# A decoder layer on one core: the first expert group's gather, and the last quarter of the output projection, cut into smaller steps

## The reference

```python
merged = gates[:, :, 0] * br_pool + gates[:, :, 1] * br_rwkv + gates[:, :, 2] * br_nsa
x = x + merged @ w_out[l]                      # the output projection
h = rms_norm(x, norm_ffn[l])
x = x + hier_moe(h, ...)                       # router, 32 experts
return rms_norm(x, norm_final)
# in hier_moe: best of 4 groups, best 2 of its 8 experts per token, then
hid = jax.nn.silu(h @ w_gate[e]) * (h @ w_up[e])
y = y + combine[..., e:e + 1] * (hid @ w_down[e])
```

## Time and profile before

| | us |
|---|---|
| median of three runs | 683.96 |
| profiled execution | 684.78 |
| its span | 683.0 |
| TensorE busy | 613.2 (90%) |
| VectorE busy | 235.7 (35%) |
| ScalarE busy | 139.6 (20%) |
| bytes moved | 158.94 MB, mean 233 GB/s |

### The profile page before, as it was taken

How to read it: one execution, slowest core, us unless ns; L and a number is a source line. 1 busy time by engine, 2 the same in 40 slices (tenths; PEclk the granted TensorE clock), 3 DMA queues, 4 the chain that set the end, 5 groups by cost and what they waited for, 6 DMA issues and landing times.

```text
span 683.0 us, 11651 instructions
## 1 busy us (share of the span) xinstructions
PE 613.2 (90%) x4900; PEld 445.8 (65%) x4900; DVE 235.7 (35%) x597; ACT 139.6 (20%) x345; POOL 22.6 (3%) x25
## 2 busy tenths in 40 slices
PE   5999999999999999999999999995888984948684
PEld 5888887888877767787778888885244441414232
DVE  2151548334254665346300222235223231213123
ACT  2110242131434442345311000001110010010013
POOL 1000000002200021000000000000000000000000
PEclk9999999999999999999999999996999997979796
DMA  9484335712201110111149964884899999999992
GB/s 346 153 323 151 124 126 190 301 62 101 87 2 64 63 63 2 63 65 54 70 164 425 421 230 176 339 342 181 341 420 418 421 419 422 421 422 421 422 390 103
DMA packets 27143, 158.94 MB, mean 233 GB/s; under 512 B 2880, under 2 KB 7120, under 8 KB 9168
## 3 DMA queue, kind: packets, MB, share of 16 engines
q1 hardware_dynamic: 24368, 139.28, 52.0%
q10 hardware_dynamic: 2720, 18.88, 6.6%
HBM read 157.07 MB, written 1.07 MB: 232 GB/s over the span
## 4 chain that ended last, share of the span: by engine, by line
PE 65%; issue 32%; ACT 1%; DVE 1%; DMA 1%; POOL 0%; SPq 0%; POOLq 0%; ACTq 0%; DVEq 0%
PE bank L601 46%; PE bank L799 5%; PE bank L897 3%; PE bank L926 2%; PE bank L946 2%; PE bank L956 1%; PE bank L910 1%; DMA table<-params 1%; PE bank L1016 1%; PE bank L831 1%; PE bank L622 1%; PE bank L861 1%; PE bank L966 1%; PE bank L850 1%; ACT ring L1482 0%
## 5 line engine op out<-in xcount | busy, mean ns | idle before, releaser
L601 PE MATMUL bank<-hT,ring 128*128 128x256 f32 (+2 forms) x960 | 216.4, 378 | 4.3 <-ACTq L1318 4.3
L601 PEld LDWEIGHTS bank<-hT,ring 128*128 128x128 f32 (+2 forms) x960 | 173.6, 190 | 37.7 <-issue 17.6
L601 PE MATMUL bank<-yT,ring 128*128 128x256 f32 x256 | 55.4, 379 | 0.0
L601 PEld LDWEIGHTS bank<-yT,ring 128*128 128x128 f32 x256 | 48.6, 190 | 6.6
L1180 PE MATMUL bank<-ring,work 128*32 128x512 f32 (+1 forms) x148 | 37.5, 680 | 16.1 <-DMA work<-experts 7.2
L1306 ACT ACTIVATE work<-bank 128x512 f32<-128x512 f32 (+1 forms) x43 | 21.8, 508 | 130.5 <-PE bank L1152 58.3
L1632 DVE TENSOR_TENSOR tok<-tok,bank 128x512 f32<-128x512 f32 (+1 forms) x34 | 22.3, 656 | 74.2 <-PE bank L1188 74.2
L1147 PEld LDWEIGHTS bank<-work 128*128 128x128 f32 x256 | 32.1, 205 | 5.5 <-issue 3.3
L1160 PE MATMUL bank<-ring,work 128*32 128x512 f32 x280 | 33.1, 594 | 1.6 <-DMA ring<-experts 1.6
L1147 PE MATMUL bank<-work 128*128 128x128 f32 x256 | 32.3, 288 | 2.0 <-DVEq L2099 2.0
L1188 PE MATMUL bank<-work 128*128 128x512 f32 (+1 forms) x68 | 33.0, 620 | 0.8 <-ACT work L1306 0.8
(11 more groups left out here) (244 smaller groups left out, 719.7 us busy)
## 6 DMA issues: line engine op xcount, KB each, us to landing
ring<-front SPq DMA_DIRECT2D x48, 1024.0 KB, 4.8
ring<-experts SPq DMA_DIRECT2D x44, 1024.0 KB, 26.5
ring<-experts ACTq DMA_DIRECT2D x8, 1024.0 KB, 11.9
table<-experts SPq DMA_DIRECT2D x6, 1024.0 KB, 26.5
yT<-experts SPq DMA_DIRECT2D x6, 1024.0 KB, 26.3
work<-experts SPq DMA_DIRECT2D x6, 1024.0 KB, 26.2
hT<-experts SPq DMA_DIRECT2D x4, 1024.0 KB, 25.5
xcmp<-experts SPq DMA_DIRECT2D x3, 1024.0 KB, 27.6
```

Source lines behind the costliest of these rows:

```text
L601: return first(pe.matmul(o, l, r, start=(k == 0), stop=(k == n - 1)))
```

## The change

Two places are rewritten.

*Last quarter.* Its tile 1 gets a PSUM bank of its own (`outlast`). VectorE adds and squares the two tiles in turn, each by itself. The transposes go into two banks, tile 0 and tile 1 apart; tile 0's are multiplied by the gain on ScalarE, tile 1's on VectorE, and `route(3)` waits for both.

*First group.* Each block's gather is followed by the gate and up products of the block before it, so the two kinds alternate. The blocks go to banks 0 and 1 in turn; ScalarE, not VectorE, multiplies each by the gain, one block at a time. The waits for `xn` and for free banks stand ahead of the one for the seats. The seats' weights are turned after the products, and ScalarE's copy of them comes after its tanh. Groups 1 to 7 keep their order; in all groups `taken` now rises with the last product of a chunk.

```diff
-        hand("out3", 7), hand("hT22", 2), hand("hT23", 3)
+        hand("out3", 7), hand("hT22", 2), hand("outlast", 6), hand("hT23", 3), hand("hTlast", 0)
...
+            def turn_last(i, name):
+                pe.wait_ge(q["sum_ready"], 4 + i)
+                o = begin(name)
+                for b in range(2):
+                    last = first(pe.transpose(o[:, b * P:(b + 1) * P], tok[:, i, (6 + b) * P:(7 + b) * P], ident))
+                end(last, name)
...
             route(2)
-            turn_sum(3)
+            turn_last(0, "hT23")
+            turn_last(1, "hTlast")
             end(route(3), "router")
...
+                def gate_up(gang, k):
+                    w = weights(gang * GCH + k).rearrange("p (e n) -> p e n", e=GANG)
+                    for e in range(GANG):
+                        last = pe.matmul(bank[2][CAP * e:CAP * (e + 1), :], gath[:, k, CAP * e:CAP * (e + 1)],
+                                         w[:, e, :], start=(k == 0), stop=(k == KD - 1))
+                    if k < KD - 1:
+                        last.then_inc(taken, 1)
+                    return last
...
+                pe.wait_ge(q["xn2_ready"], NT)
+                for j in range(8):
+                    pe.wait_ge(bank_free[j], before_loop[j])
+                pe.wait_ge(q["sel_ready"], 1)
+                for k in range(KD + 1):
+                    if k < KD:
+                        gather(bank[k % 2][:, k // 2 * P:(k // 2 + 1) * P], k).then_inc(q["gathered"], 1)
+                    if k:
+                        pe.wait_ge(q["gath_ready"], k)
+                        last = gate_up(0, k - 1)
...
# ScalarE, ahead of its xn copies
+            b0 = full(act, "hT23")
+            for k in (6, 7):
+                ins = copy(hT[:, k, 0:P], b0[:, (k - 6) * P:(k - 5) * P], scale=pr("g_ffn")[:, k:k + 1])
+            give(ins, "hT_odd_ready", "hT23")
# ScalarE, gathered_experts
+                for k in range(KD):
+                    act.wait_ge(q["gathered"], k + 1)
+                    copy(gath[:, k, :], bank[k % 2][:, k // 2 * P:(k // 2 + 1) * P], scale=pr("g_ffn")[:, k:k + 1])\
+                        .then_inc(q["gath_ready"], 1)
...
# VectorE
-            for n in range(4):
+            for n in range(3):
...
+            for i, name in enumerate(("out3", "outlast")):
+                b0 = full(dve, name)
+                o = tok[:, i, 768:D]
+                chain(stt(o, b0[:, i * 256:(i + 1) * 256], 0.5, o, ALU.mult, ALU.add), "sum_ready")
+                dve.sem_inc(bank_free[plan[name][0]], 1)
+                squares(o, stat[:, 27 + 4 * i:28 + 4 * i], at=256 * i)
...
-            sum_turned(3)
+            b0 = full(dve, "hTlast")
+            chain(tt(hT[:, 6:8, P:S], b0[:, 0:2 * P].rearrange("p (k t) -> p k t", k=2),
+                     like(pr("g_ffn")[:, 6:8, None], [P, 2, P]), ALU.mult), "hT_ready")
+            dve.sem_inc(bank_free[plan["hTlast"][0]], 1)
```

More of the change, by code:

```diff
@@ L1061, in output @@
                 w = chunk(C_OUT + n).rearrange("p (k c) -> p k c", k=KD)
-                o = begin(f"out{n}") if 0 in tiles else bank[plan[f"out{n}"][0]]
+                name = "outlast" if tiles == (1,) else f"out{n}"
+                o = begin(name)
                 for i in tiles:
@@ L1067, in output @@
                         last = mm(o[:, i * 256:(i + 1) * 256], merged[:, k, i * P:(i + 1) * P], w[:, k, :], k, KD)
+                end(last, name)
                 if 1 in tiles:
-                    end(last, f"out{n}")
                     pe_take()
@@ L1079, in turn_sum @@
                 end(last, f"hT2{n}")
+            def turn_last(i, name):
+                pe.wait_ge(q["sum_ready"], 4 + i)
+                o = begin(name)
+                for b in range(2):
+                    last = first(pe.transpose(o[:, b * P:(b + 1) * P], tok[:, i, (6 + b) * P:(7 + b) * P], ident))
+                end(last, name)
             def route(n):
+                if n == 3:
+                    pe.wait_ge(q["hT_odd_ready"], 3)
                 pe.wait_ge(q["hT_ready"], 2 + n + 1)
@@ L1134, in gathered_experts, with gather, turn_weights @@
             def gathered_experts():
[L1137 to L1149, removed]
+                def gate_up(gang, k):
[6 more added lines that the diff above has]
+                    return last
+                def gather(o, k):
+                    for i in range(NT):
+                        last = pe.matmul(o, xn[:, i, k * P:(k + 1) * P], sel[:, i, :], start=(i == 0), stop=(i == 1))
+                    return last
+                def turn_weights(gang):
                     pe.wait_ge(q["wsel_ready"], gang + 1)
@@ L1153, in gathered_experts @@
                     last.then_inc(q["wsel_turned"], 1)
[L1155 to L1163, removed]
+                pe.wait_ge(q["xn2_ready"], NT)
[8 more added lines that the diff above has]
+                        last = gate_up(0, k - 1)
+                for gang in range(NGANG):
+                    if gang:
+                        pe.wait_ge(q["sel_ready"], gang + 1)
+                        for b in range(2):
+                            for kk in range(4):
+                                last = gather(bank[b][:, kk * P:(kk + 1) * P], 4 * b + kk)
+                            last.then_inc(q["gathered"], 1)
+                        turn_weights(gang)
+                        for k in range(KD):
+                            if k % 4 == 0:
+                                pe.wait_ge(q["gath_ready"], KD + (gang - 1) * 2 + (k // 4 + 1))
+                            last = gate_up(gang, k)
                     last.then_inc(q["gate_up"], 1)
+                    if gang == 0:
+                        turn_weights(0)
                     if gang == NGANG - 1:
@@ L1575, in gathered_experts @@
             def gathered_experts():
+                for k in range(KD):
+                    act.wait_ge(q["gathered"], k + 1)
+                    copy(gath[:, k, :], bank[k % 2][:, k // 2 * P:(k // 2 + 1) * P], scale=pr("g_ffn")[:, k:k + 1])\
+                        .then_inc(q["gath_ready"], 1)
                 for gang in range(NGANG):
-                    act.wait_ge(q["wsel_turned"], gang + 1)
-                    copy(wselT, bank[3][:, 2 * P:4 * P].rearrange("p (i t) -> p i t", i=2)).then_inc(q["wselT_ready"], 1)
+                    if gang:
+                        act.wait_ge(q["wsel_turned"], gang + 1)
+                        copy(wselT, bank[3][:, 2 * P:4 * P].rearrange("p (i t) -> p i t", i=2)).then_inc(q["wselT_ready"], 1)
                     act.wait_ge(q["gate_up"], gang + 1)
                     act.activation(gtanh, bank[2][:, 0:DE], ACT.Tanh, scale=0.5).then_inc(q["gtanh_ready"], 1)
+                    if gang == 0:
+                        act.wait_ge(q["wsel_turned"], 1)
+                        copy(wselT, bank[3][:, 2 * P:4 * P].rearrange("p (i t) -> p i t", i=2)).then_inc(q["wselT_ready"], 1)
                     if gang == NGANG - 1:
@@ L2135, in gathered_experts @@
                 for gang in range(NGANG):
-                    for b in range(2):
-                        dve.wait_ge(q["gathered"], gang * 2 + b + 1)
+                    for b in range(2 if gang else 0):
+                        dve.wait_ge(q["gathered"], KD + (gang - 1) * 2 + b + 1)
                         tt(gath[:, 4 * b:4 * b + 4, :], bank[b][:, :].rearrange("p (k s) -> p k s", k=4),
```

## The result

The changed kernel takes 679.22 us (median of six runs, 676.25 to 681.08) against 684.28 for the kernel before (six runs, 682.13 to 685.11): a ratio of 0.9923, 95% interval 0.9894 to 0.9952. Run again beside other kernels it gave 0.9920 (0.9899 to 0.9941). So it is faster by 0.5 to 1.1%, about 5 us; 5.5 were forecast. The profiled execution took 681.08 us, its span is 679.3.

The account below looks back on a forecast made before the run. The expert-weight stream, and when it starts, was taken to bound the kernel. 0.85 + 4.65 = 5.5 us off the profiled 684.78 gave 679.3 (678.5 against the median); range 676.5 to 680.5, 8 in 10 676.0 to 681.6.

Parts of the forecast that it names:

- What sets the end: Expert-weight stream to the kernel's end: each microsecond by which chunk 22 is issued earlier should come off the time.
- The quarter: Last output quarter: splitting the work by tile brings the seats 0.85 us earlier, bounds 0.61 to 0.9.
- The first release: First expert group: chunk 22 goes out 3.65 us after the seats, at 474.35 against 479.86, all at the low clock.
- the 4.65: First expert group: the 4.65 us summed with the quarter's 0.85 to give 5.5 us off.
- The chunk's cost: First group on TensorE: a gather and products cost 2.56 us per chunk at the low clock, 1.28 at full.
- The rival without the stream: End does not follow the stream: only the first group's earlier end counts, 1.3 us, time 682.7; chance 8%.
- Is the stream fed: Weight loads after chunk 22: second issue in time within 0.1 us; chunks 8 to 11 back near 491.0, before 495.9.
- No gap: Weight stream near 496: eight chunks keep the DMA engines going until 495.9, with chunks 8 to 11 back near 491.0.
- The rest: Stretch after the last chunk's landing: a fixed chain of 19.6 us, about 2 us shorter at full clock.
- ScalarE was not late: Rival, first group: ScalarE's first copy comes late after the branch, first release slips some 1.7 us, time 680.2; chance 8%.
- The low clock did not stay: Rival, first group: alternation keeps the clock at 1.2 GHz, the stream stands still some 8.4 us, time 686.9; chance 5%.

Follow-up runs that it names:

- the run with two chunks held: Changed kernel, but SyncE issues chunk 22 only once three chunks of the first group are used, not one; ratio 0.9962 to the kernel before.
- the run with nine matmuls: Changed kernel plus matmuls whose result nobody reads, seven after the router and two ahead of the branch; ratio 0.9926 to the kernel before.
- the run with seven chunks held: Changed kernel, but SyncE issues chunk 22 only when chunk 7 of the first group is given back too; ratio 1.0114 to the kernel before.

## Why the prediction was right

**What sets the end.** Right, and shown: 7.75 us more at the issue made 7.77 at the landing and 7.8 (6.1 to 9.4) in the time. An earlier issue counts less what the stream then loses: 5.26 at the issue made 3.9 to 5.2 at the landing.

**The quarter.** 0.85 was forecast; the first gather comes 0.80 earlier with it than without it (11.78 against 12.58 with the first group changed in both), and the logits 0.79 (3.29 for 4.08). ScalarE's two copies began where forecast, 1.10 after the end of the output projection, and took 0.62, not 0.57 (a single one takes 0.37, not 0.29). They were over at 460.87, VectorE's gain at 461.16, and the router's matmuls began at 461.27.

**The first release.** 3.65 after the seats was forecast; it took 3.98 in each of the three traces, all at the low clock as assumed. The difference is mostly the step from the second gather to the first products: 1.98 after the first gather, not 1.70. The issue came 5.26 earlier, not 5.5. (The 8.31 from which the 4.65 comes is counted from the seats; from the gather of before it is 8.28.)

**The chunk's cost.** This term was mis-sized: a gather and its products were taken at the sum of their durations, 1.28, and cost 1.64. So, and by the longer low clock below, the first group's products end 15.5 after the first gather, not 13.0, and in the pair of profiles 1.4 us later than before rather than 1.3 earlier. The rival without the stream would have had a slower kernel by this; the stream hid it, since chunks 8 to 11, back at 493.67, were wanted by about 496.

**Is the stream fed.** "No gap" was too simple. The low clock lasted to about 476.8, 5.9 us after the gather (5.0 was assumed); over the 4 us from 474.91 it averaged 0.77. The second load went out 2.5 us after the first, and the stream lost 0 to 1.4 us from issue to landing. With the issue 5.26 earlier, the landing was 3.9, 5.2 and 4.5 earlier in three traces. Where this loss comes from stays open. It is 0.05 or less in all four kernels whose first loads follow each other in under 1 us, and 0 to 2.7 where the first two go out 1.6 or more apart, which speaks for the slow release; but one such trace has none of it, and the loss does not lie where the release is slowest. Summed over the stretches, every one of the twelve traces had moved about 1 MB (0.97 to 1.06) 4 us after the issue of chunk 22, whenever the second load went out. Over the next 4 us the five traces without loss came to 2.69 to 2.73 MB, the others only to 2.25 to 2.58; the changed kernel had 2.47 in the first trace, by when five chunks (5.2 MB) had been issued. So in the dip there were loads to move, and no run here shows what held them.

**The rest.** It was called fixed at 19.6, with 2 us less at full clock and as much to be lost. It was 16.4 to 16.8 in seven traces, 19.4 to 19.6 in four and 20.9 in one, by the clock that TensorE is granted after its wait for the last landing: 0.50 in the first trace of the changed kernel, 1.00 in the run with two chunks held.

```profile
662.00:664.00 2.00, 1.22 (x5) 0.50 (x2) 0.00 (x0) 0.60 (x1) 0.00 (x0) 0.50 0.74 240
```

```profile
664.00:666.00 2.00, 1.33 (x3) 0.68 (x4) 0.20 (x1) 0.52 (x1) 0.00 (x0) 1.00 0.99 315
```

The pair of profiles, both with the long rest, differs by 3.7 us: 3.85 at the landing and 0.16 in the rest, less the 0.31 by which this execution began the stage later. The medians differ by 5.06. That they come so near to the 5.5 is in part luck: the three landings of the changed kernel are only 4.5 earlier on average, and its rest was 2.9 shorter in two of them. How often the kernel before has the short rest, its one trace can't say.

**The rivals.** ScalarE was not late: its first copy began 1.24 after the first gather at the low clock and 0.72 after it at full clock (472.56 in the run with nine matmuls), with the gather's own 0.85 and 0.43 in that. The low clock did not stay: it rose in the middle of the alternating group. The Trainium skill (TensorE: Matmul & The Clock Gate, "Loop structure matters more than you think") warns of a long wait for DMA between matmuls, on which the engine goes cold; no such wait shows in this group, where TensorE was busy all the time from 471 to 480.

## What to carry to other kernels

Where weights stream to the end, look for the event that lets the first load go after the buffers are full; time saved there is saved at the end, less what the stream then loses, and work on TensorE behind it may even get longer as long as the next buffers come back before the queue runs dry. Cost an alternation of two kinds of matmul by a row that has the change between them in it, not by the sum of the two. And an earlier first load need not be worth its full lead: a further 2.2 us at the issue brought nothing here, and why the stream was slower then stays open.

## What was not expected of the hardware

A change between float32 matmuls over the whole 128-column array and matmuls on four strips of 32 columns costs about 0.36 us for there and back (1.64 for 1.28 at full clock; 2.95 for two chunks).

Matmuls that nobody reads kept TensorE's clock at 2.4 GHz up to the gather in one run and not in another: the run with TensorE idle from 469.90 to 471.25 had 1.2 GHz at the gather, the run with it idle from 471.18 to 471.84 had 2.4 GHz.

A stream of 1 MB loads issued into an idle queue took about 2 us to come to its rate, whether one load was out or several: in the 2 us behind the first issue 0.21 MB were moved in the changed kernel (one load out), 0.19 in the kernel before (three) and 0.16 in the run with seven chunks held (four). From 476.91 to 477.41 us the changed kernel moved 377 GB/s, before its second load went out at 477.46.
